# Mix, routing and experts in one block: logits and squares computed tile by tile, the row factor applied later

## The chip, the cores and the metric

One NeuronCore of one Trainium2 chip runs the whole program. The metric is the device time of one execution in microseconds; the kernel before takes 1579.05 us (median of 3 runs, 1575.91 to 1585.28).

## The reference

One inference step of two layers over 264 tokens (256 of a prompt, 8 of decode) of width 1024. Each layer adds four gated branches and then a hierarchical mixture of experts. The change touches the end of the first and the start of the second:

```
proj  = einsum('ntbw,bwd->ntbd', branches, w_branch)      # 4 branches of width 256
gates = sigmoid(gate_raw)                                 # 4 x 1024 a token
x = x + einsum('ntbd,ntbd->ntd', gates, proj) @ w_out

h  = x * rsqrt(mean(x*x) + eps) * norm2_g
pg = softmax(h @ moe_wg + moe_bg)                         # 4 groups, the best one is taken
le = (h @ moe_we + moe_be) of the 8 experts of that group # the best two are taken
e_w = softmax weights of the two, normed to 1, times pg of the group
y = sum over the two of  e_w * (silu(h @ w_gate) * (h @ w_up)) @ w_down   # 1024 -> 256 -> 1024
x = x + y
```

## The kernel before, in words

Activations are kept with features on partitions: `xT`, `hT` are 128 x 8 x 264 (8 tiles of 128 features, 264 tokens). All matrix products are float32 matmuls of TensorE, which the program issues as two instructions each; some operands are split into a high and a low `float32r` part instead, which are multiplied apart.

Each layer is a row of blocks: project, mla, gdn, memory, `mix`, `moe`. A block hands each engine its own list of instructions; engines meet through semaphores, and a barrier of all engines stands between blocks. Loads go out on SyncE's queue (SP) in program order; a wait in that order holds back everything behind it.

`mix` (L1737) loops over the 8 feature tiles `dt`: TensorE multiplies the branches with `w_br` (L1776), VectorE multiplies with the sigmoid of the gates and sums the four branches into `mixT` (L1814 to L1821). Then the output loop (L1784 to L1791) multiplies `mixT` with the 8 tiles of `w_out`, 8 matmuls of 264 columns a tile; VectorE adds each tile to `xT` (L1828). The first four tiles of `w_out` are loaded at the start of the block, tile 4 + i when tile i has been multiplied (L1765).

`moe` (L1847) starts with the loads of the expert weights: pieces of 128 x 1024 floats (512 KB). Tokens are sorted into 48 slots of 32 rows: two of three slots belong to an expert for good (base, 192 pieces of six per slot), the third takes the overflow of whichever expert has more than 32 tokens (96 pieces). Base pieces go round a ring of 21 buffers, overflow pieces round a ring of 3; an overflow piece is loaded only when its slot is used, by a DMA with a condition read from `items` into registers (L1928, L1929, L1931). When a chunk has been multiplied (`chunk_done`), SP issues the base loads that its buffers allow and then the overflow loads.

Ahead of the experts comes a serial chain. VectorE squares `xT` (L2207), TensorE sums over features with a matrix of ones (L1997), ScalarE takes the root, VectorE the reciprocal and `hT = xT * g2 * rstd` (L2213). TensorE computes the 36 logits for three thirds of 88 tokens (L2004), VectorE splits `hT` into high and low (L2217, L2221), TensorE turns the split tiles so that tokens lie on partitions (`split_turn`, L2016, 12 groups of 4 transposes; three groups of four), and ScalarE copies them to `hTM` (L2165). VectorE picks group and experts (`first_max`), TensorE counts tokens per expert and ranks them (L2025, L2029), VectorE finds each token's slot (three `pick`s, L2268, and some small operations) and writes the selection matrix `G` for the first two quads of slots (L2289, L2290). After that come, in TensorE's order, four gathers `hTM` x `G` (L2043), the table of the overflow slots (L2112, computed by VectorE in L2293 to L2299), the transposed slot numbers (L2115), and the first expert chunk. ScalarE copies gathered rows to `HS` (L2174).

The expert stage goes through 12 quads of four slots: four chunks gate/up (L2067), SiLU on ScalarE (L2189), times the up half and the slot's weight `wS` on VectorE (L2339), two transposes (L2076), two chunks down (L2083), `Y` split on ScalarE and VectorE, and 8 matmuls that scatter `Y` back to tokens (L2096), added to `xT` on VectorE (L2332). In between, the gathers for the next two quads run, with `G` from GpSimd (L1967, L1970) and the scatter matrix `Q` from GpSimd (L1978, L1981).

Of the kernel before, what the change touches and what calls it, by code (L numbers as in the profile page):

```python
# [6 lines left out]

# [15 lines left out]
P = 128  # L23
# [43 lines left out]
                  stri=128, sub=1, cols=GCOLS, valid=3, slot=QUADS, quad=QUADS + 1, first=NE, thr=T // W,  # L67
# [25 lines left out]
def constants():  # L93
# [41 lines left out]
    put("first", np.broadcast_to(W * (3 * (e // 2) + e % 2), (P, NE)))  # L135
    put("thr", np.broadcast_to(W * np.arange(1, T // W + 1), (P, T // W)))
# [8 lines left out]
def build(nc, A):  # L145

    with ExitStack() as top:
# [3 lines left out]
        xT = alloc(top, "xT", [P, KT, T])  # L151
        hT = alloc(top, "hT", [P, KT, T])
# [1584 lines left out]
def mix(nc, A, E, l, F):  # L1737

    xT, brT, bank = (E[k] for k in ("xT", "brT", "bank"))
    g0, gT = F["g0"], F["gT"]  # L1740
    with E["Phase"]("mix") as ph:
        S = ph.sem
        w = F["wbr"]
        wo = [ph.sb(f"wo{i}", [P, KT, P]) for i in range(4)]
        mixT = ph.sb("mixT", [P, KT, T])

        def gates(dt, b, n):

            first = 4 * dt + b
            if isinstance(dt, int):  # L1750
                return (g0 if first < MLA_TILES else gT)[:, first % MLA_TILES:first % MLA_TILES + n, :]
            return gT[:, bass.ds(first - MLA_TILES, n), :]

        @ph.b.sync
        def _(sp):
            for i in range(4):
                sp.dma_start(wo[i][:], A["w_out"][l, i]).then_inc(S(f"wo{i}_loaded"), 16)
            with sp.Fori(1, KT // 2) as i:
                for s in range(2):
                    src = A["w_br"][l, 2 * i + s]  # L1760
                    sp.wait_ge(S(f"p{s}_done"), 4 * i)
                    sp.dma_start(w[s][:], src).then_inc(S(f"w{s}_loaded"), 16)
            for i in range(4):
                sp.wait_ge(S("o_done"), i + 1)
                sp.dma_start(wo[i][:], A["w_out"][l, 4 + i]).then_inc(S(f"wo{i}_loaded"), 16)  # L1765

        @ph.b.tensor
        def _(pe):
            def pair(i):
                for s in range(2):  # L1770
                    if not isinstance(i, int):
                        pe.wait_ge(S(f"w{s}_loaded"), 16 * i)
                        pe.wait_ge(S(f"p{s}_read"), 4 * i)
                    for b in range(4):
                        for k in range(2):
                            mm = pe.matmul(bank[4 * s + b][:, 0:T], w[s][:, 2 * b + k, :], brT[:, 2 * b + k, :],  # L1776
                                           start=k == 0, stop=k == 1)
                        mm.then_inc(S(f"p{s}_done"), 1)

            pair(0)  # L1780
            with pe.Fori(1, KT // 2) as i:
                pair(i)
            pe.wait_ge(S("mix_ready"), KT)
            for dt in range(KT):  # L1784
                i = dt % 4
                pe.wait_ge(S(f"wo{i}_loaded"), 16 * (dt // 4) + 16)
                if dt >= 4:
                    pe.wait_ge(S("x_ready"), dt - 3)
                for k in range(KT):
                    mm = pe.matmul(bank[i][:, 0:T], wo[i][:, k, :], mixT[:, k, :], start=k == 0, stop=k == KT - 1)  # L1790
                mm.then_inc(S("o_done"), 1)  # L1791

        @ph.b.scalar
        def _(act):
            def sigmoid(dt):
                nc.scalar.activation(gates(dt, 0, 4), gates(dt, 0, 4), ACT.Sigmoid).then_inc(S("gates_ready"), 1)
# [644 lines left out]
```

## Time and profile before

| | |
|---|---|
| median of 3 runs | 1579.05 us |
| the profiled execution | 1595.82 us, span 1594.0 us |
| busy share of the span | PE 83%, PEld 58%, DVE 45%, ACT 20%, POOL 11% |
| granted TensorE clock | 0.914 of full speed |
| moved by DMA | 307.93 MB, mean 193 GB/s |

PE is TensorE's matmuls, PEld its weight loads, DVE VectorE, ACT ScalarE, POOL GpSimd, SPq the queue of SyncE. The clock is a share of full speed; its two levels are 1.2 and 2.4 GHz. The two layers run the same program, and the span covers both; the first layer's output loop begins at 478.4 us and its experts end at 799.0.

### The profile page before, as it was taken

To read this page: it belongs to the slowest core of one execution; us is meant where nothing else is said; L and a number is where in the kernel's file an instruction comes from. 1 tells how busy PE (TensorE), PEld (TensorE's weight loads), DVE (VectorE), ACT (ScalarE), POOL (GpSimd) and SP (SyncE) were. 2 spreads that over 40 slices of the span, in tenths; PEclk is the share of its full clock that TensorE was granted. 3 is DMA by queue.
4 is the path that set the end of the run, shared out by engine and by line. 5 is a ranking of instruction groups with operands and counts; after the bars stand their busy time and mean duration, and the time that the engine had idled before them with its cause. 6 is when DMAs were issued, how large, how long until landed. Compare 5 with 4: busy or idle time off the path is not lost. (4 is left out here: it accounts for less than half of the span.)

```text
span 1594.0 us, 23230 instructions
## 1 busy us (share of the span) xinstructions
PE 1330.4 (83%) x8322; PEld 928.4 (58%) x8322; DVE 724.4 (45%) x1479; ACT 318.6 (20%) x610; POOL 176.7 (11%) x182
## 2 busy tenths in 40 slices
PE   5968978977889799888879689789788888897886
PEld 2946856966467644343249468579665775443342
DVE  3654766365451612222247547564654534222222
ACT  0212614111120221111111126131111203111110
POOL 0040000000000133330000400000000002333310
PEclk9998989978899699999979989899789997999999
DMA  5462022126133589999734520221261356899995
GB/s 190 150 207 66 1 44 80 53 79 234 58 132 110 229 331 409 408 408 408 288 118 159 198 66 0 55 70 53 79 245 47 132 177 231 343 408 409 408 408 234
DMA packets 89962, 307.93 MB, mean 193 GB/s; under 512 B 16368, under 2 KB 19200, under 8 KB 88192
## 3 DMA queue, kind: packets, MB, share of 16 engines
q1 hardware_dynamic: 86784, 296.08, 49.9%
q0 software_dynamic: 3072, 10.49, 1.9%
q8 instruction: 60, 0.98, 0.3%
q14 instruction: 46, 0.38, 0.1%
HBM read 403.21 MB, written 3.98 MB: 255 GB/s over the span
## 5 line engine op out<-in xcount | busy, mean ns | idle before, releaser
L499 PE MATMUL bank<-hT,wf 128*128 128x264 f32 x1024 | 254.5, 407 | 34.7 <-PEq L202 19.5
L499 PEld LDWEIGHTS bank<-hT,wf 128*128 128x128 f32 x1024 | 203.6, 202 | 78.7 <-issue 26.5
L2067 PE MATMUL bank<-moe_wover,moe_scr 128*32 128x512 f32 x512 | 193.2, 632 | 34.4 <-DMA moe_wover<-in_w_gu 34.1
L2067 PE MATMUL bank<-moe_wbase,moe_scr 128*32 128x512 f32 x1024 | 194.2, 622 | 5.1 <-DMA moe_wover<-in_w_gu 5.1
L2332 DVE TENSOR_TENSOR xT<-xT,bank 128x264 f32<-128x264 f32 x192 | 73.4, 425 | 168.1 <-PE bank L2096 168.1
L2043 PEld LDWEIGHTS bank<-moe_G,moe_hTM 88*128 88x128 f32 x576 | 81.5, 209 | 82.2 <-issue 68.4
L2043 PE MATMUL bank<-moe_G,moe_hTM 88*128 88x256 f32 x576 | 99.2, 316 | 11.7 <-DVE moe_G L2290 9.0
L2083 PE MATMUL bank<-moe_wover,moe_acT 128*32 128x512 f32 x256 | 91.8, 607 | 14.0 <-DMA moe_wover<-in_w_d 10.3
L2083 PE MATMUL bank<-moe_wbase,moe_acT 128*32 128x512 f32 x512 | 91.9, 613 | 9.9 <-ACT moe_acT L2194 6.5
L267 DVE TENSOR_TENSOR moe_Y<-bank,moe_Y 128x512 fp32r<-128x512 f32 x48 | 30.9, 686 | 137.2 <-ACT moe_Y L2197 137.2
L1960 POOL MEMSET moe_wover<- 128x3072 f32 x2 | 5.3, 2658 | 792.4 <-DMA wf<-in_w_gate 792.4
L2174 ACT COPY moe_scr<-bank 128x256 f32<-128x256 f32 x96 | 35.8, 372 | 227.8 <-PE bank L2043 227.8
L2067 PEld LDWEIGHTS bank<-moe_wover,moe_scr 128*32 128x32 f32 x512 | 40.4, 113 | 66.2 <-issue 65.3
L2067 PEld LDWEIGHTS bank<-moe_wbase,moe_scr 128*32 128x32 f32 x1024 | 41.7, 112 | 60.7 <-issue 54.3
L1978 POOL TENSOR_SCALAR moe_Gt<-moe_rows,cst 128x528 f32<-128x528 f32 x24 | 38.5, 1602 | 303.7 <-PE bank L2096 291.4
L1776 PE MATMUL bank<-brT,wbr 128*128 128x264 f32 x256 | 62.6, 405 | 7.1 <-PEq L202 4.4
L2096 PE MATMUL bank<-moe_Q,moe_Y 128*128 128x264 f32 x384 | 64.8, 292 | 2.9 <-DVE moe_Y L267 2.8
L273 PE MATMUL bank<-proj_hsp,proj_wsp 128*128 128x264 f32 x224 | 64.6, 288 | 1.9 <-DVE proj_wsp L267 1.9
L1967 POOL TENSOR_SCALAR moe_Gt<-cst,moe_shifted 88x256 f32<-88x256 f32 x60 | 55.5, 935 | 76.4 <-DVE moe_shifted L2306 73.6
L2096 PEld LDWEIGHTS bank<-moe_Q,moe_Y 128*128 128x128 f32 x384 | 52.8, 189 | 19.1 <-issue 11.7
L274 PE MATMUL bank<-proj_hsp,proj_wsp 128*128 128x264 f32 x224 | 63.5, 283 | 0.0
L275 PE MATMUL bank<-proj_hsp,proj_wsp 128*128 128x264 f32 x224 | 63.5, 283 | 0.0
(509 smaller groups left out, 2150.9 us busy)
## 6 DMA issues: line engine op xcount, KB each, us to landing
moe_wbase<-in_w_gu SPq DMA_DIRECT2D x256, 512.0 KB, 12.3
moe_wbase<-in_w_d SPq DMA_DIRECT2D x128, 512.0 KB, 12.6
moe_wover<-in_w_gu SPq DMA_DIRECT2D x128, 512.0 KB
wf<-in_w_gate SPq DMA_DIRECT2D x64, 512.0 KB, 3.5
moe_wover<-in_w_d SPq DMA_DIRECT2D x64, 512.0 KB
proj_wfm<-in_w_fm SPq DMA_DIRECT2D x28, 512.0 KB, 3.4
wbr<-in_w_br SPq DMA_DIRECT2D x16, 512.0 KB, 3.5
mix_wo<-in_w_out SPq DMA_DIRECT2D x16, 512.0 KB, 5.0
```

The lines of the kernel that those rows point to most:

```text
L273: pe.matmul(out, wh, xh, start=start, stop=False)
L274: pe.matmul(out, wh, xl, start=False, stop=False)
L275: return pe.matmul(out, wl, xh, start=False, stop=stop)
L499: mm = pe.matmul(E["bank"][to][:, 0:T], F["wf"][slot][:, k, :], E["hT"][:, k, :], start=k == 0, stop=k == KT - 1)
L1776: mm = pe.matmul(bank[4 * s + b][:, 0:T], w[s][:, 2 * b + k, :], brT[:, 2 * b + k, :], start=k == 0, stop=k == 1)
L1967: nc.gpsimd.tensor_scalar(Gt[0:n, i, 0:GCOLS], C("cols")[0:n], shifted[0:n, g, i, c:c + 1], None, ALU.is_equal).then_inc(S("gt_ready"), 1)
L1978: nc.gpsimd.tensor_scalar(Gt[:], rows[:], C("slot")[:, q:q + 1], None, ALU.is_equal)\
L2043: mm = pe.matmul(bank[to][:, 0:GCOLS], h[0:n, c, P * k:P * k + P], G[g % 2][0:n, c, :], start=part == 0 and c == 0, stop=part == 1 and c == 2)
L2067: mm = pe.matmul(bank[0][W * p:W * p + W, :], HS[q // GROUP % 2][:, k, at + W * p:at + W * p + W], w[p][:, 512 * (k % 2):512 * (k % 2) + 5 ...
L2083: mm = pe.matmul(bank[2 + half][W * p:W * p + W, :], acT[:, f, W * p:W * p + W], w[p][:, 512 * half:512 * half + 512], start=f == 0, stop= ...
L2096: mm = pe.matmul(bank[4 + n % 3][:, 0:T], Y[part][:, P * d:P * d + P], Q[:, q % 2, :], start=part == 0, stop=part == 1)
L2332: tt(x, x, bank[4 + n % 3][:, 0:T], ALU.add).then_inc(S("x_ready"), 1)
```

## The change

`mix` and `moe` become one block, `tail`, without a barrier between them. The features of the new `x` are scaled by the gain alone (`xg`), not by the row factor 1/rms. Behind the fourth matmul of each output tile, TensorE adds the previous tile's contribution to a 37 x 264 sum: 36 logits of `xg`, and the sum of squares in row 37 (`logits`). `xg` is split and half of the transpose groups run inside the loop. The 37 rows are then turned to tokens on partitions, and the row factor is applied to the logits there; later it enters as a second set of slot weights: SiLU takes it as its scale, and the weight that multiplies the up half contains it as well. The gather goes by thirds as `G` is written. The overflow table is computed on GpSimd right after the offsets, its matmul stands before the gather, and the conditional loads move from SP to ScalarE. The base pieces are loaded in the output loop, into memory that gates and branches held; the memory of `w_out` is later that of the overflow pieces, and `mixT` uses `hT`.

```diff
-def mix(nc, A, E, l, F):
+def tail(nc, A, E, l, F):
...
+            sp.dma_start(wrt[:], A["w_rt"][l]).then_inc(S("wrt_loaded"), 16)
             for i in range(4):
                 sp.dma_start(wo[i][:], A["w_out"][l, i]).then_inc(S(f"wo{i}_loaded"), 16)
...
+            sp.wait_ge(S("mix_ready"), KT)
             for i in range(4):
                 sp.wait_ge(S("o_done"), i + 1)
                 sp.dma_start(wo[i][:], A["w_out"][l, 4 + i]).then_inc(S(f"wo{i}_loaded"), 16)
+                for nb in range(5 * i, 5 * i + 5):
+                    load(nb)
+            for nb in range(20, BASE_RING):
+                load(nb)
...
+        def _(pool):
+            pool.wait_ge(S("o_done"), KT)
+            nc.gpsimd.memset(wover[:], 0.0).then_inc(S("cleared"), 1)
+            pool.wait_ge(S("off_ready"), 2)
+            nc.gpsimd.tensor_tensor(ncnt[:, 2:3], ncnt[:, 3:4], ncnt[:, 1:2], ALU.add).then_inc(S("table_step"), 1)
...
+            nc.gpsimd.tensor_scalar(table[:, 0], table[:, 1], C("eidx")[0:NE], None, ALU.mult)\
+                .then_inc(S("table_ready"), 1)
...
+            def logits(k):
+                pe.wait_ge(S("sq_ready"), k + 1)
+                pe.matmul(bank[4][0:37, 0:T], last[:], sq[:, k % 2, :], start=k == 0, stop=False).then_inc(S("ss_done"), 1)
+                pe.wait_ge(S("xg_ready"), k + 1)
+                pe.matmul(bank[4][0:37, 0:T], wrt[:, k, :], xg[:, k % 3, :], start=False, stop=k == KT - 1).then_inc(S("lg_done"), 1)
...
             pe.wait_ge(S("mix_ready"), KT)
+            pe.wait_ge(S("wrt_loaded"), 16)
+            pe.wait_ge(S("zeroed"), 1)
             for dt in range(KT):
...
                 for k in range(KT):
                     mm = pe.matmul(bank[i][:, 0:T], wo[i][:, k, :], mixT[:, k, :], start=k == 0, stop=k == KT - 1)
+                    if k == 3 and dt:
+                        logits(dt - 1)
                 mm.then_inc(S("o_done"), 1)
+                if 4 <= dt < 7:
+                    split_turn(2 * dt - 8)
+                    split_turn(2 * dt - 7)
+            logits(KT - 1)
+            split_turn(6)
+            pe.wait_ge(S("lgT_ready"), 1)
             for c, (t0, n) in enumerate(THIRDS):
+                mm = pe.transpose(bank[4][0:n, 37 * c:37 * c + 37], lgT[:, t0:t0 + n], ident[0:37, 0:37])
+            mm.then_inc(S("lgT_done"), 1)
+            for b in range(7, 12):
+                split_turn(b)
...
-            split_turn(2)
+            pe.wait_ge(S("table_ready"), 1)
+            pe.matmul(bank[1][:, 0:2 * OVER], ones[0:NE, :], table[:].rearrange("p a b -> p (a b)"), start=True,
+                      stop=True).then_inc(S("items_done"), 1)
...
-            pe.wait_ge(S("G_ready"), 3)
             pe.wait_ge(S("hTM_ready"), 12)
-            for k in range(4):
-                gather(0, k, 4 + k)
-            pe.wait_ge(S("table_ready"), 1)
...
+            for c, (t0, n) in enumerate(THIRDS):
+                pe.wait_ge(S("G_ready"), c + 1)
+                for k in range(4):
+                    for part, h in enumerate(hTM):
+                        mm = pe.matmul(bank[4 + k][:, 0:GCOLS], h[0:n, c, P * k:P * k + P], G[0][0:n, c, :],
+                                       start=part + c == 0, stop=part + c == 3)
...
+            nc.scalar.activation(rs[:, 3:4], E["epsc"][:], ACT.Sqrt)
+            for dt in range(KT):
+                act.wait_ge(S("res_ready"), dt + 1)
...
+                nc.scalar.activation(sq[:, dt % 2, :], xT[:, dt, :], ACT.Square).then_inc(S("sq_ready"), 1)
+                if 4 <= dt < 7:
+                    turned(2 * dt - 8)
+                    turned(2 * dt - 7)
...
+            def refill(n):
+                act.wait_ge(S("chunk_done"), n + 1)
+                for i in range(OVER_RING, len(over_pieces)):
+                    if last_user(over_pieces[i - OVER_RING]) == n:
+                        load(i)
+            act.wait_ge(S("items_ready"), 1)
+            act.wait_ge(S("cleared"), 1)
+            for i in range(OVER_RING):
+                load(i)
             for k in range(KT):
                 gathered(0, k, 4 + k % 4)
+                if k == 5:
+                    refill(0)
+            refill(1)
...
+                for c in range(3 if q else 0):
+                    if more:
                         gathered(g + 1, 4 * (q % GROUP) + c, 7)
+                    refill(STEPS * q + c)
+                if q == 0:
+                    refill(2)
+                    act.wait_ge(S("wS_ready"), 1)
                 act.wait_ge(S("chunk_done"), STEPS * q + 4)
-                nc.scalar.activation(sg[:], bank[0][:, 0:256], ACT.Silu).then_inc(S("silu_done"), 1)
+                nc.scalar.activation(sg[:], bank[0][:, 0:256], ACT.Silu, scale=wS[:, 1, q:q + 1])\
+                    .then_inc(S("silu_done"), 1)
...
+            for dt in range(KT):
+                dve.wait_ge(S("o_done"), dt + 1)
+                x = xT[:, dt, :]
+                tt(x, x, bank[dt % 4][:, 0:T], ALU.add).then_inc(S("res_ready"), 1)
...
+                ts(xg[:, dt % 3, :], x, V("g2", dt), None, ALU.mult).then_inc(S("xg_ready"), 1)
...
+                high_part(nc, hsp[0][:, dt, :], xg[:, dt % 3, :]).then_inc(S("h_high"), 1)
...
+                low_part(v, hsp[1][:, dt, :], xg[:, dt % 3, :], hsp[0][:, dt, :]).then_inc(S("h_split"), 1)
+            step(v.tensor_copy(lgT[:], bank[4][0:37, 0:T]), "lgT_ready", wait=False)
+            dve.wait_ge(S("root_ready"), 1)
+            step(v.reciprocal(rs[some, 0:3], rs[some, 0:3]))
...
-            step(tt(ohg[:], ohg[:], C("valid").unsqueeze(2).to_broadcast([P, 3, 4]), ALU.mult))
             for i in range(2):
-                for c in range(3):
-                    step(tt(OH[:, i, c].rearrange("p (g e) -> p g e", g=4),
-                            ohg[:, c].unsqueeze(2).to_broadcast([P, 4, 8]),
-                            oh[i][:, c].unsqueeze(1).to_broadcast([P, 4, 8]), ALU.mult), wait=i + c == 3)
+                step(tt(OH[:, i].rearrange("p c (g e) -> p c g e", g=4),
+                        ohg[:].unsqueeze(3).to_broadcast([P, 3, 4, 8]),
+                        oh[i][:].unsqueeze(2).to_broadcast([P, 3, 4, 8]), ALU.mult), wait=i == 1)
...
-PHASES = [branches, moe]
+PHASES = [branches]
```

## Rows read from the trace of the kernel before

**Rows 1.** Windows, layer 0: us, busy time (instructions) by engine, PEclk, DMA share, GB/s.
```profile
478.40:508.90 30.50, 30.44 (x128) 25.35 (x128) 3.02 (x8) 0.00 (x0) 0.00 (x0) 0.94 0.24 70
...
542.90:552.00 9.10, 6.54 (x31) 5.89 (x32) 3.44 (x18) 1.49 (x4) 1.54 (x2) 0.50 0.00 0
...
566.20:579.60 13.40, 11.51 (x74) 6.91 (x74) 0.65 (x2) 2.46 (x7) 11.41 (x13) 0.75 0.67 247
579.60:785.20 205.60, 177.66 (x1416) 80.19 (x1408) 51.15 (x116) 32.77 (x78) 46.36 (x47) 0.97 1.02 405
785.20:799.00 13.80, 10.57 (x78) 4.89 (x74) 6.11 (x15) 1.83 (x4) 0.00 (x0) 1.00 0.04 17
```

**Rows 2.** Timeline, output loop to turning, layer 1: start, length, operation, [idle before, releaser].
```profile
1278.45 0.43 DVE L1828 TENSOR_TENSOR xT<-xT,bank 128x264 f32<-128x264 f32 x1 [3.13 <-PE bank L1790]
...
1299.81 0.43 DVE L1828 TENSOR_TENSOR xT<-xT,bank 128x264 f32<-128x264 f32 x1 [3.13 <-PE bank L1790]
...
1317.34 0.19 DVE L2224 TENSOR_TENSOR moe_lg<-bank,row 88x36 f32<-88x36 f32 x1 [1.34 <-PE bank L2004]
...
1325.23 1.95 PE L2016 MATMUL bank<-cst,moe_scr 128*88 128x128 f32 x16
```

**Rows 3.** Groups by line and form, VectorE: busy us, mean ns of one.
```profile
L1555 DVE TENSOR_SCALAR gdn_y<-zT,vec 128x264 f32<-128x264 f32 x12 | 3.4, 351 | 5.6 <-PEq L202 5.6
...
L2269 DVE TENSOR_REDUCE moe_tq<-moe_Aq 128x6 f32<-128x192 f32 x6 | 2.1, 353 | 0.2
```

**Rows 4.** Timeline, logits to the first expert chunk, layer 0.
```profile
528.09 0.19 DVE L2224 TENSOR_TENSOR moe_lg<-bank,row 88x36 f32<-88x36 f32 x1 [1.33 <-PE bank L2004]
...
532.70 0.70 DVE L2250 TENSOR_TENSOR moe_OH<-moe_ohg,moe_oh 128x32 f32<-128x32 f32 x6
...
540.51 0.48 DVE L2290 SCALAR_TENSOR_TENSOR moe_G<-cst,moe_tq,moe_Gt 88x256 fp32r<-88x256 f32 x1
...
542.32 0.48 DVE L2290 SCALAR_TENSOR_TENSOR moe_G<-cst,moe_tq,moe_Gt 88x256 fp32r<-88x256 f32 x1
...
542.85 5.49 PE L2043 MATMUL bank<-moe_G,moe_hTM 88*128 88x256 f32 x24 [4.02 <-DVE moe_G L2290]
...
548.83 0.60 PE L2115 MATMUL bank<-cst,moe_tq 88*2 88x88 f32 x3
549.47 0.42 DVE L2301 COPY moe_tokT<-bank 2x264 f32<-2x264 f32 x1 [5.34 <-PE bank L2115]
...
551.67 0.81 SPq L1931 DMA_DIRECT2D moe_wover<-in_w_gu  x3
...
551.99 1.07 PE L2067 MATMUL bank<-moe_wbase,moe_scr 128*32 128x512 f32 x2 [2.56 <-DMA moe_wover<-in_w_gu]
```

**Rows 5.** Timeline, layer 0: the table on VectorE, GpSimd's first and third pair.
```profile
543.19 0.22 DVE L2296 TENSOR_SCALAR moe_table<-cst,moe_ncnt 32x16 f32<-32x16 f32 x1
...
550.46 2.28 POOL L1967 TENSOR_SCALAR moe_Gt<-cst,moe_shifted 88x256 f32<-88x256 f32 x2 [37.65 <-DVE moe_shifted L2306]
...
556.45 1.82 POOL L1967 TENSOR_SCALAR moe_Gt<-cst,moe_shifted 88x256 f32<-88x256 f32 x2
```

**Rows 6.** Chain of work that ended last, layer 1, first and second expert chunk.
```profile
1341.26 3.64 PE bank L2067 x16
...
1346.92 1.85 PE bank L2067 x16
```

**Rows 7.** Timeline, end of the experts, layer 0.
```profile
775.01 0.08 SPq L1931 DMA_DIRECT2D moe_wover<-in_w_d  x1
775.17 0.59 PE L2083 MATMUL bank<-moe_wbase,moe_acT 128*32 128x512 f32 x1 [1.80 <-DMA moe_wover<-in_w_d]
...
796.08 2.89 DVE L2332 TENSOR_TENSOR xT<-xT,bank 128x264 f32<-128x264 f32 x8
```

**Rows 8.** Timeline, first SiLU, layer 0: the table load, the slot weights.
```profile
565.13 1.28 ACT L2189 ACT_TABLE_LOAD   x1
...
567.75 0.17 DVE L2327 COPY moe_wS<-bank 128x12 f32<-128x12 f32 x1 [13.88 <-PE bank L2133]
```

More of the change, by code:

```diff
@@ L8 @@
+import math
 from contextlib import ExitStack
@@ L1863, in moe, with at @@
     over_at = {x: i for i, x in enumerate(over_pieces)}
[L1864 removed]
+    with E["Phase"]("tail") as ph:
         S = ph.sem
[L1866 to L1868 removed]
+        where = [-(-F["at"] // 32) * 32]
+        def at(name, shape, dt=F32):
+            t = nc.alloc_sbuf_tensor_at(f"tail_{name}", shape, dt, offset=where[0])
+            where[0] += -(-4 * math.prod(shape[1:]) // 32) * 32
+            return t
+        wbase = at("wbase", [P, BASE_RING, D_MODEL])
+        where[0] = -(-max(where[0], F["end"]) // 32) * 32
+        again = where[0]
+        wo = [at(f"wo{i}", [P, KT, P]) for i in range(4)]
+        above = where[0]
+        mixT = hT
+        where[0] = again
+        wover = at("wover", [P, OVER_RING, D_MODEL])
+        sg = at("sg", [P, 256])
+        ac = at("ac", [P, 256])
+        acT = at("acT", [P, 2, P])
+        assert where[0] <= above
+        where[0] = above
+        Y = [nc.alloc_sbuf_tensor_at(f"tail_Y{i}", [P, D_MODEL], F32R, offset=E["hT_at"] + 4 * D_MODEL * i)
+             for i in range(2)]
+        scr = at("scr", [P, 2 * KT * T])
@@ new lines, in tail @@
+        Q = at("Q", [P, 2, T], F32R)
+        rows = at("rows", [P, 2, T])
+        wS = at("wS", [P, 2, QUADS])
+        rs = at("rs", [P, 4])
+        last = at("last", [P, 37])
+        lgT = at("lgT", [37, T])
+        wrt = at("wrt", [P, KT, 37])
+        lg = at("lg", [P, 3, 36])
+        m = at("m", [P, 8, 3])
+        eg = at("eg", [P, 3, 4])
+        ohg = at("ohg", [P, 3, 4])
+        sel = at("sel", [P, 3, 4, 8])
+        le = at("le", [P, 3, 8])
+        oh = [at(f"oh{i}", [P, 3, 8]) for i in range(2)]
@@ L2020, in _, with pair @@
-            pe.wait_ge(S("h_split"), 4)
-            split_turn(0)
-            split_turn(1)
+            def pair(i):
+                for s in range(2):
+                    if not isinstance(i, int):
+                        pe.wait_ge(S(f"w{s}_loaded"), 16 * i)
+                        pe.wait_ge(S(f"p{s}_read"), 4 * i)
+                    for b in range(4):
+                        for k in range(2):
+                            mm = pe.matmul(bank[4 * s + b][:, 0:T], w[s][:, 2 * b + k, :], brT[:, 2 * b + k, :],
+                                           start=k == 0, stop=k == 1)
+                        mm.then_inc(S(f"p{s}_done"), 1)
@@ L2348, in _, with branches @@
                 add(KT * (QUADS - 1) + d)
-PHASES = [branches, moe]
+def branches(nc, A, E, l):
+    with ExitStack() as shared:
+        sb = lambda name, shape: E["alloc"](shared, name, shape, F32)
+        base = nc.sbuf_base
+        g0 = sb("g0", [P, MLA_TILES, T])
+        E = dict(E, zT=sb("zT", [P, FM_N, T]), tm=sb("tm", [P, 3, TM_W]), brT=sb("brT", [P, 8, T]))
+        F = dict(g0=g0, wf=[sb(f"wf{i}", [P, KT, P]) for i in range(2)])
+        project(nc, A, E, l, F)
+        mla(nc, A, E, l, dict(F, gT=g0, at=0))
+        F.update(gT=sb("gT", [P, GATE_TILES - MLA_TILES, T]), memT=sb("memT", [P, KT, MEM]))
+        gdn(nc, A, E, l, dict(F, at=0))
+        F.update(wbr=[sb(f"wbr{i}", [P, 8, P]) for i in range(2)])
+        F.update(end=nc.sbuf_base)
+        memory(nc, A, E, l, dict(F, at=GDN_TILES))
+        tail(nc, A, E, l, dict(F, at=base))
+PHASES = [branches]
 OUTS = dict(
```

434 lines of the change are left out of this document (181 added, 253 removed).

## The prediction

> **What bounds the kernel now.** I read the windows over the stages of the first layer first, then the timelines around the hand-over from the output loop to the experts, then the chain of waits for the second layer. From the first refill to the last landing, 205.6 us of the expert stage run with the 16 DMA engines fully busy at 405 GB/s, while TensorE is busy 177.66 us of it [rows 1]: the stream of expert weights sets this stage. Ahead of it the stream stands still: between 542.9 and 552.0 nothing moves [rows 1], because the ring of 21 base pieces is full and no expert chunk has been computed. So the end of a layer follows the moment at which the first expert chunk frees a buffer; everything that brings this chunk forward by 1 us brings the end forward by 1 us, as long as the stream behind it is the same. That chunk stands at the end of one serial chain: output loop, barrier, square sums, logits, routing on VectorE, gather, overflow table, loads. After the last landing 13.8 us of computing are left [rows 1].
>
> **Output loop to logits.** The loop goes at 3.56 us a tile (0.43 of the residual add and 3.13 idle before it) [rows 2], so 16 instructions at 0.2225. In layer 0 loop start to biased logits is 478.4 to 528.28, 49.9 us [rows 1, 4]; in layer 1 the loop ends at 1299.81, started 28.5 earlier, and the logits end at 1317.53: 46.2 us [rows 2]. All square sums, the normalisation, its split and the old logits lie in that.
> The change puts two more matmuls of 264 columns behind each tile but the last: 4 instructions, 0.89 us, seven times, 6.2 us on TensorE's own path. Six of the twelve transpose groups move into the loop as well, 24 transposes at 1.95/16 = 0.12 [rows 2], 3.0 us. VectorE does four operations of 264 columns per tile (0.43, 0.35 [rows 3], two more of that kind) and ScalarE one square and at times two copies, under 2 us of each 4.45 us tile: hidden behind TensorE. After the last tile stand the add 0.43, the gain 0.35, two matmuls 0.89, the copy out of PSUM 0.42 [rows 4], three small transposes, one copy and the root on ScalarE, reciprocal, scale and bias, with some eight hand-overs of 0.1: 4.6 us, between 4 and 6.5 (the upper end if ScalarE has to load its table once more, 1.28 [rows 8]). New length: layer 0 30.4 + 6.2 + 3.0 + 4.6 = 44.2, a gain of 5.7; layer 1 28.5 + 6.2 + 3.0 + 4.6 = 42.3, a gain of 3.9. Together 9.6.
> Against it: TensorE now waits for two memsets on VectorE before the loop, 0.35, and the routing weights stand first on SP's queue and push the w_br loads back by 0.35: 1.4 for both layers.
> SP's queue in the loop: the second half of w_out goes out one tile at a time with five base pieces of 512 KB behind each, 1.3 us a piece at the 405 GB/s of the full stream [rows 1]. The last w_out piece lies behind 18 others and lands some 30 us into the loop; its tile starts at 33. This hides it by 3 us. The window of the loop shows 70 GB/s now [rows 1], so there is room. That the base pieces come 30 us earlier is worth nothing by itself: the ring is full before routing ends in both kernels.
>
> **Routing to the first expert chunk.** The mask and six one-hot writes (0.70 [rows 4]) become two wider writes: 0.4 gained, bounds 0 to 0.9. Six slot operations shrink to four, one copy is added: 0.35 gained, bounds 0 to 0.6. The gather now starts on the first third of G instead of the third: 540.51 + 0.48 = 540.99 instead of 542.80 [rows 4]. From 540.99 - 0.75 = 540.24 its 24 matmuls take 5.49, to 545.7; the three transposes 0.60, to 546.4. Before, the table matmul stood behind the gather, then the copies to integers, SP's register loads and its issue at 551.67, and the first expert matmul ran at 551.99 [rows 4]. Now the table is done while VectorE builds G, and ScalarE, idle there, issues the loads. Gain 5.6 a layer, 11.2 together.
> What this hangs on is GpSimd. Five operations of 16 columns on it, each waiting for the one before, precede the table matmul (0.56), and TensorE stands in order behind that matmul, with the whole gather. VectorE meanwhile has two picks (0.35 for each half [rows 3]), six small operations and the first pair of G, some 3.4 us. No row has such an operation on GpSimd: VectorE's for the same table is 0.22, GpSimd's for 256 columns is 1.14 or 0.91 [rows 5]. That gives 1.6 to 6.2 us with hand-overs, so a loss of 0 to 3.4 a layer. 16 columns are nearer to the small one: I take 2.5 us and no loss.
> The pair of GpSimd at 550.46, beside a busy VectorE, took 2.28; the pair at 556.45, beside an idle one, 1.82 [rows 5]. The Trainium skill, page "SBUF — State Buffer", section "SBUF: two separate sides", says that VectorE in some kinds of operation and GpSimd lock one shared port pair for a whole instruction; by the rule each of the five could wait for one VectorE operation, about 1.7 us in all, and the table would still come about with G; by the row the price is 0.23 an operation. The trace agrees in sign; neither changes the sum.
> Clock: the first chunk runs at half clock in both layers, 3.64 us for 16 matmuls against 1.85 soon after [rows 6], after 2.5 us without work for TensorE. That pause goes. Gain 0 to 2.6 a layer with the gathers beside it; I take 1.3, together 2.6.
> First SiLU: ScalarE now waits for the slot weights (567.92) before it; the table load that stood at 565.13 [rows 8] may come behind this wait, and the gathers' copies behind that: 0 to 1.3 lost a layer, 0.6 taken, together 1.2.
>
> **Expert stage.** The same pieces at the same rate: no change over 205.6 us. ScalarE gets 96 conditional loads a layer, and 16 times two register loads. Behind each stand its own copies of gathered rows, SiLU, Y. In a quad with two overflow slots the load for the next chunk is issued behind a gather's copy, so TensorE may wait some 0.5 us, 12 times, 6 us a layer, beside 27.9 us of slack: hidden by the stream.
> The tail is different. SP issues the overflow loads in order behind base loads that it can't place: one came out at 775.01 and TensorE, idle for 1.80 us, started at 775.17 [rows 7]. So TensorE is several chunks behind the stream when it ends at 785.2. On ScalarE's queue a skipped load is done at once, and TensorE can follow the landings: the last down chunk and part of the one before, 3 us, and 5.4 of Y, its low part and the combine (the last eight adds alone 2.89 [rows 7]) give 8.4 after the last landing, instead of 13.8: up to 5.4, or nothing if TensorE is late for other reasons. I take 3 a layer, together 6.
>
> **Sum.** 9.6 - 1.4 + 11.2 (which holds the 0.75 a layer of the routing) + 2.6 - 1.2 + 6 = 26.8, say 27 us of the profiled execution's 1595.82 (span 1594.0). That execution is 1% above the median of the runs, 1579.05; I take the difference off the median: 1552. With every term at its low end 5 us are left, with every one at its high end 38.
>
> **Rivals.**
> *Given back before the experts* (about 1573): GpSimd at its upper price (6.8 for both layers), ScalarE's table load behind the root (2.6) and behind the slot weights (1.4 more), nothing from the tail (6), the clock (2.6) or the shorter routing (1.5): 20.9 of the 27 are gone. For it: TensorE is in order behind the table; against it: 256 columns are no measure for 16. Chance 0.13.
> *The clock falls in the expert stage* (slower, 1605). Now that TensorE isn't held in lumps, it would follow the stream in small gaps. Place: the 205.6 us of each layer. Price: a chunk at half clock takes 3.64 for 1.85 [rows 6], so each us at half clock costs 0.5. It decides from 56 us a layer on, where the slack of 27.9 is used up; at half the stage, 103 us, it costs 23.5 a layer: 47 less the 21 that are left of the gain. For it: from 566.2 to 579.6 TensorE was busy 11.51 of 13.4 us and the granted clock was 0.75, between its levels of 1.2 and 2.4 GHz. Against it: over the long stage it was busy the same share and had 0.97 [rows 1]. The Trainium skill, page "TensorE: Matmul & The Clock Gate", section "HAM oscillation — how this bites in real kernels", has this mechanism: a kernel that waits for DMA between bursts of matmuls loses its clock again and again. The trace has it in the one stretch and not in the other. Chance 0.07.
> *ScalarE becomes the bound* (about 1590): if a conditional load cost it over 0.7 us in the chain of each chunk, 27.9 us of slack over 40 chunks would be gone. SP's three loads took 0.81 [rows 4], so 0.27 each. Chance 0.08.
>
> **How the numbers follow.** Forecast 0.72, its own range 1544 to 1571. The range of 1541 to 1577 takes in most of the first rival and holds some 8 in 10. Within 0.5% of 1579 (1571 to 1587) is what a measurement of this kernel can't tell from no change: faster 0.77, the same 0.12, slower 0.11.
>
> **What will show it.** The output loop with 4.45 us between its adds; first add after the loop to biased logits under 6 us; the first expert matmul some 10 us sooner after the loop's start; DMA idle only in routing; 205 us of full DMA as before; 8 to 9 us after the last landing. Wrong if the table matmul starts after the first third of G, if TensorE's waits for base pieces come with a clock under 0.9 in the long stage, or if that stage is longer than 208 us.

## The result, and the profile after

The changed kernel takes 1573.22 us (median of 20 runs, 1560.37 to 1583.53), the kernel before, run beside it, 1582.56 us (20 runs): ratio 0.9942, interval 0.9919 to 0.9964. It is faster by 9 us (0.6%), not by the 27 of the forecast. The profiled execution took 1580.17 us (span 1578.4) against 1595.82: 15.6 us between the spans. The stretches that the change touches hold 9.2 of these. Another 7.5 lie in the blocks ahead of them, whose code is the same: the first branch matmul comes 3.1 us earlier in layer 0, and in layer 1 4.4 us more than the end of layer 0 did. Behind the experts of layer 1, 1.1 us are lost again.

Windows of layer 0 after, columns as in [rows 1] (busy time of PE, PEld, DVE, ACT, POOL, then PEclk, DMA share, GB/s):

```profile
440.70:478.50 37.80, 32.89 (x128) 26.13 (x129) 22.31 (x53) 10.62 (x11) 0.00 (x0) 0.91 0.44 143
478.50:520.00 41.50, 41.48 (x180) 29.84 (x180) 10.74 (x29) 5.83 (x13) 0.00 (x0) 0.96 0.80 316
520.00:526.40 6.40, 3.95 (x18) 2.40 (x18) 4.57 (x8) 1.32 (x4) 2.66 (x1) 0.78 0.00 0
526.40:538.40 12.00, 6.49 (x40) 5.86 (x38) 8.49 (x43) 4.17 (x8) 1.51 (x5) 0.64 0.01 1
538.40:545.30 6.90, 5.95 (x30) 5.49 (x30) 2.59 (x8) 1.46 (x4) 0.00 (x0) 0.50 0.00 0
545.30:565.00 19.70, 18.32 (x124) 10.21 (x124) 5.18 (x21) 5.05 (x12) 15.47 (x17) 0.85 0.78 292
565.00:573.00 8.00, 7.49 (x44) 3.10 (x48) 0.00 (x0) 0.74 (x2) 5.00 (x6) 0.60 0.29 94
573.00:777.50 204.50, 177.38 (x1432) 81.16 (x1424) 51.94 (x118) 33.73 (x78) 46.46 (x47) 1.00 1.02 407
777.50:789.04 11.54, 8.24 (x58) 3.96 (x54) 5.34 (x13) 1.92 (x4) 0.00 (x0) 1.00 0.05 20
```

One line for each stretch of the serial path: branch tiles, output loop, end of the logits, routing, gather, first quad (two lines), stream, tail. The loop has TensorE busy for all of its 41.5 us; the stream runs as before, at 407 GB/s with the full clock.

The same stretches, cut at the starts of instructions in the timelines (the biased logits and the experts at their ends), in us for layer 0 / layer 1; forecast and measured are gains over both layers:

| stretch | before | after | forecast | measured |
|---|---|---|---|---|
| first branch matmul to first output matmul | 34.6 / 34.5 | 37.8 / 37.8 | -1.4 | -6.5 |
| to the last residual add | 30.5 / 28.8 | 41.5 / 41.5 | -18.4 | -23.8 |
| to the biased logits | 19.4 / 17.7 | 6.4 / 6.4 | +27.9 | +24.4 |
| to VectorE's first operation for G | 11.8 / 11.9 | 12.0 / 12.0 | +1.5 | -0.3 |
| to the first expert matmul | 11.9 / 11.9 | 6.8 / 6.8 | +9.7 | +10.0 |
| to the end of the experts | 247.0 / 245.7 | 243.8 / 243.4 | +7.4 | +5.5 |
| sum | 355.2 / 350.5 | 348.3 / 348.0 | +26.7 | +9.2 |

Timeline after, end of the output loop in layer 0:

```profile
520.06 0.43 DVE L2251 TENSOR_TENSOR xT<-xT,bank 128x264 f32<-128x264 f32 x1 [4.02 <-PE bank L1970]
520.09 2.66 POOL L1881 MEMSET tail_wover<- 128x3072 f32 x1 [401.81 <-PE bank L1970]
520.53 2.37 DVE L2255 TENSOR_SCALAR tail_xg<-xT,vec 128x264 f32<-128x264 f32 x1
522.95 0.64 PE L1944 MATMUL bank<-tail_xg,tail_wrt 128*37 128x264 f32 x2 [1.31 <-DVE tail_xg L2255]
523.75 1.08 PE L1954 MATMUL bank<-cst,tail_scr 128*88 128x128 f32 x4 [0.16 <-DVE tail_scr L270]
526.15 0.27 DVE L2267 TENSOR_TENSOR tail_lg<-tail_lg,row 88x108 f32<-88x108 f32 x1
```

The last gain operation takes 2.37 us, where the same operation takes 0.36 in the loop. GpSimd's memset of the overflow buffers began beside it, also released by the last output tile.

### The profile page after: what moved, and what is told of

Same layout as the page of the kernel before. It is cut to its first block and busy times, and to the rows that moved or that the text cites. A ratio compares the mean times of both kernels' runs of the same rounds, so it can differ in the third digit from the quotient of the medians.

```text
span 1578.4 us, 23156 instructions
## 1 busy us (share of the span) xinstructions
PE 1331.3 (84%) x8264; PEld 921.3 (58%) x8264; DVE 722.7 (46%) x1485; ACT 327.1 (21%) x628; POOL 183.0 (12%) x192
## 3 DMA queue, kind: packets, MB, share of 16 engines
q0 software_dynamic: 3072, 10.49, 1.9%
## 5 line engine op out<-in xcount | busy, mean ns | idle before, releaser
L2032 PE MATMUL bank<-tail_wbase,tail_scr 128*32 128x512 f32 x1024 | 186.4, 604 | 21.2 <-DMA tail_wbase<-in_w_gu 21.2
L2032 PE MATMUL bank<-tail_wover,tail_scr 128*32 128x512 f32 x512 | 185.4, 601 | 4.5 <-DMA tail_wbase<-in_w_gu 4.5
L2048 PE MATMUL bank<-tail_wbase,tail_acT 128*32 128x512 f32 x512 | 94.9, 622 | 22.2 <-DMA tail_wbase<-in_w_d 14.7
L2008 PEld LDWEIGHTS bank<-tail_G,tail_hTM 88*128 88x128 f32 x528 | 70.3, 196 | 68.5 <-issue 64.1
L2048 PE MATMUL bank<-tail_wover,tail_acT 128*32 128x512 f32 x256 | 94.6, 613 | 7.6 <-ACT tail_acT L2210 3.8
L2008 PE MATMUL bank<-tail_G,tail_hTM 88*128 88x256 f32 x528 | 87.8, 305 | 2.8 <-ACT tail_scr L2160 2.8
L1970 PE MATMUL bank<-hT,tail_wo 128*128 128x264 f32 x256 | 65.6, 408 | 4.7 <-DVE tail_last L2244 4.7
L2061 PE MATMUL bank<-tail_Q,tail_Y 128*128 128x264 f32 x384 | 65.5, 295 | 2.9 <-DVE tail_Y L270 2.8
L1935 PEld LDWEIGHTS bank<-brT,wbr 128*128 128x128 f32 x256 | 52.5, 208 | 22.3 <-issue 12.2
L2061 PEld LDWEIGHTS bank<-tail_Q,tail_Y 128*128 128x128 f32 x384 | 53.8, 191 | 18.9 <-issue 11.7
```

The costliest lines, as they stand in the source:

```text
L2008: mm = pe.matmul(bank[to][:, 0:GCOLS], h[0:n, c, P * k:P * k + P], G[g % 2][0:n, c, :], start=part == 0 and c == 0, stop=part == 1 and c == 2)
L2032: mm = pe.matmul(bank[0][W * p:W * p + W, :], HS[q // GROUP % 2][:, k, at + W * p:at + W * p + W], w[p][:, 512 * (k % 2):512 * (k % 2) + 5 ...
L2048: mm = pe.matmul(bank[2 + half][W * p:W * p + W, :], acT[:, f, W * p:W * p + W], w[p][:, 512 * half:512 * half + 512], start=f == 0, stop= ...
L2061: mm = pe.matmul(bank[4 + n % 3][:, 0:T], Y[part][:, P * d:P * d + P], Q[:, q % 2, :], start=part == 0, stop=part == 1)
```

## The experiments

All change the changed kernel unless said; ratios are against the kernel before, run on the same chip. Where a whole time can't separate two kernels, the stretches of the table do; each is read from one execution with two layers.

**The changed kernel again.**

> The changed kernel itself once more, beside the others on the same chip, for the size of what the parts gave: 0.994 of the time before, first branch matmul to the end of the experts 348 us in each layer. If its routing counts at full clock in this execution (1.9 instead of 3.3 us), 1.4 less.

1575.22 us, 0.9952 (0.9923 to 0.9981). From the first branch matmul to the end of the experts (branch to end, below) 346.9 / 346.8. Counting, from the one-hot rows to the ranks, took 3.27 us in layer 0 and 1.90 in layer 1; the branch stretch 36.5 and 38.2: these two move with the granted clock from one execution to the next.

**Routing weights last.**

```diff
-            sp.dma_start(wrt[:], A["w_rt"][l]).then_inc(S("wrt_loaded"), 16)
             for i in range(4):
                 sp.dma_start(wo[i][:], A["w_out"][l, i]).then_inc(S(f"wo{i}_loaded"), 16)
             with sp.Fori(1, KT // 2) as i:
...
+            sp.dma_start(wrt[:], A["w_rt"][l]).then_inc(S("wrt_loaded"), 16)
             sp.wait_ge(S("mix_ready"), KT)
```

> The changed kernel with one load moved: the routing weights (148 KB in 148-byte rows) go out behind the branch-weight refills instead of ahead of w_out. Theory (the load holds back the refills): the second pair of branch tiles waits 2.24 us in the changed kernel and runs at half clock (9.07 us instead of 7.38); without the load ahead the wait falls to the 0.9 to 1.1 us of the kernel before and the second pair to 7.4, so first branch matmul to first output matmul is 35.0 us instead of 37.8 in both layers, some 5.5 us in all: 1567 to 1568. Rival (the refills are held by the four w_out tiles alone, the changed kernel's longer wait has another cause): the wait stays over 2 us, the time at 1573.

1566.38 us, 0.9928 (0.9900 to 0.9957). Timeline of the branch tiles in layer 0, first the changed kernel, then this one:

```profile
440.79 0.33 SPq L1850 DMA_DIRECT2D tail_wrt<-in_w_rt  x1
...
451.99 9.03 PE L1935 MATMUL bank<-brT,wbr 128*128 128x264 f32 x32 [2.24 <-DMA wbr<-in_w_br]
```

```profile
444.82 14.97 PE L1935 MATMUL bank<-brT,wbr 128*128 128x264 f32 x64 [0.96 <-DMA wbr<-in_w_br]
```

In layer 0 the wait falls to 0.96, and two pairs of tiles take 14.97, where one took 9.03 in the changed kernel. In layer 1 the wait is long, 2.76, but only because the first pair ran at full clock there (7.36 us instead of 9.04):

```profile
1212.46 7.36 PE L1935 MATMUL bank<-brT,wbr 128*128 128x264 f32 x32 [2.09 <-PEq L205]
1222.58 22.68 PE L1935 MATMUL bank<-brT,wbr 128*128 128x264 f32 x96 [2.76 <-DMA wbr<-in_w_br]
```

In both layers the second pair begins 10.0 to 10.1 us after the first, as in the kernel before (9.9 to 10.2); in the eight runs that have the load ahead it is 10.5 to 12.6, in the changed kernel 11.3. The stretch is 34.9 / 35.1, as in the kernel before. So the load costs what its landing delays, and what TensorE's clock loses in the wait, not its 0.33 us of issue. The share of the clock differs between executions: in the changed kernel run again, layer 0, the second pair waited 2.71 us and still ran at full clock (7.38). Counting, too, ran at full clock in both layers (1.90). The rows of this load are not of 148 bytes: the array holds the 8 x 37 floats of a partition in one piece, 1184 bytes.

**Clearing in the loop.**

```diff
-            pool.wait_ge(S("o_done"), KT)
-            nc.gpsimd.memset(wover[:], 0.0).then_inc(S("cleared"), 1)
+            for i in range(OVER_RING):
+                pool.wait_ge(S("o_done"), 5 + i)
+                nc.gpsimd.memset(wover[:, i], 0.0).then_inc(S("cleared"), 1)
```

> The changed kernel, with GpSimd's clearing of the three overflow buffers cut into three pieces of 1024 columns, each behind the output tile that used this memory last (the fifth, sixth and seventh), instead of one piece of 3072 behind the eighth. Theory (GpSimd's memset holds VectorE's gain operation that starts beside it): the last xg takes 0.36 us instead of 2.37, last add to biased logits 4.4 us instead of 6.36, 2 us a layer, 4 in all: 1569; single operations inside the loop get longer by up to 0.9 and stay hidden. Rival (the last xg is long because it waits for something else): 2.37 stays, 1573.

1568.43 us, 0.9940 (0.9910 to 0.9969): as a whole not to be told from the changed kernel. In the profiled execution the branch stretch of layer 1, which this edit doesn't touch, took 40.3. The edited stretch is clear: last add to biased logits 4.18 in both layers, 2.2 less. Timeline of layer 0, a tile with a memset and the last:

```profile
501.95 0.95 POOL L1882 MEMSET tail_wover<- 128x1024 f32 x1 [387.74 <-PE bank L1971]
...
502.39 0.66 DVE L2256 TENSOR_SCALAR tail_xg<-xT,vec 128x264 f32<-128x264 f32 x1
...
519.33 0.36 DVE L2256 TENSOR_SCALAR tail_xg<-xT,vec 128x264 f32<-128x264 f32 x1
```

Each piece beside a gain operation lengthens it, to 0.66; alone it takes 0.36. In both kernels it ends 0.15 us after the memset does (522.90 after 522.75; 503.05 after 502.90). The Trainium skill, page "SBUF — State Buffer", section "SBUF: two separate sides", says that the port pair shared by GpSimd and VectorE (in some of VectorE's kinds of operation) is locked for a whole instruction by whichever of the two engines starts first; by that rule VectorE waits out the memset, and these rows agree, but for the end: 0.15 us behind the memset is less than the 0.36 that the operation takes alone.

**All turns behind the logits.**

```diff
-                if 4 <= dt < 7:
-                    split_turn(2 * dt - 8)
-                    split_turn(2 * dt - 7)
             logits(KT - 1)
-            split_turn(6)
...
-            for b in range(7, 12):
+            for b in range(12):
                 split_turn(b)
```

> The changed kernel with all twelve transpose groups behind the three small transposes of the logits, none in the output loop and none ahead of the logits. Theory (they cost TensorE's path there, and behind the logits TensorE has nothing else to do): output loop 41.5 to 38.9 us, the group ahead of the small transposes gives 0.7, and counts and ranks run at full clock (1.83 us instead of 3.2) because TensorE works right up to them: 4.7 us a layer, 9 in all, 1564. Rival (TensorE, at half clock, gets through twelve groups only after VectorE has its one-hot rows, and counting starts late): first half gained, 1 to 2 us a layer given back, 1568 to 1570. Rival 2 (the loop was bound by the loads of w_out and pieces): loop stays at 41.5, 1573.

1565.54 us, 0.9908 (0.9876 to 0.9941). Loop 37.2 / 39.4 (full clock / first tiles at half clock), last add to logits 5.5 instead of 6.4, counting 1.90 / 1.89. Timeline of layer 0:

```profile
522.38 5.90 PE L1954 MATMUL bank<-cst,tail_scr 128*88 128x128 f32 x48
...
528.54 0.35 PE L1984 MATMUL bank<-ones,tail_both 88*32 88x1 f32 x6 [0.27 <-DVE tail_both L2286]
```

The twelve groups fit between the logits and the one-hot rows; TensorE then stands idle for 0.27 us instead of 2.98, and counts at full clock. With the turns in the loop, in seven runs, counting ran at full clock throughout in 4 of 14 layers, at half in 5; with all turns behind the logits, in five runs, at full in all ten.

**Overflow loads back on SP.**

```diff
-                act.dma_start(wover[:, i % OVER_RING], source(e, c), cond=used)
+                sp.dma_start(wover[:, i % OVER_RING], source(e, c), cond=used)
```

(with the order of SP of the kernel before)

> The changed kernel with the conditional overflow loads back on SP, in the order of the kernel before; all else as changed. Theory (ScalarE's queue lets TensorE follow the landings): the tail after the last landing goes back from 11.5 to 13.8 us in the first layer, TensorE's waits for base pieces turn into waits for overflow loads again: 2 to 3 us a layer slower, 1577 to 1579. Rival (the loads on ScalarE cost as much as they give, they stand ahead of its copies in the first quads): the same within 2 us, 1572 to 1575. Rival 2 (they hold up ScalarE more than they give): faster, 1568.

1578.07 us, 0.9987 (0.9960 to 1.0015). First expert matmul to the end 246.9 / 245.5, as before the change (247.0 / 245.7). TensorE's waits by releaser (us, times, longest), changed kernel, then this one:

```profile
PE bank L2032 <- DMA tail_wbase<-in_w_gu: 25.7, 28, 1.9
PE bank L2048 <- DMA tail_wbase<-in_w_d: 14.7, 10, 1.8
```

```profile
PE bank L2051 <- DMA tail_wover<-in_w_gu: 31.1, 21, 6.1
PE bank L2067 <- DMA tail_wover<-in_w_d: 12.6, 9, 1.7
```

So without the move to ScalarE the expert stage keeps only 0.3 of the 5.5 us that it gained.

**Wide weights.**

```diff
-        last = at("last", [P, 37])
+        last = at("last", [P, P])
-        wrt = at("wrt", [P, KT, 37])
+        wrt = at("wrt", [P, KT, P])
```

(columns 37 to 127 cleared at the start of the block)

> The changed kernel with the weights of the logits and of the square sums padded with zeros to 128 columns (two buffers of xg instead of three to make room). In the changed kernel a tile with logits takes 4.77 us: 16 w_out instructions 3.76 and four for the logits 1.01, against 3.56 and 0.89 at the pace of the loop before. Theory (weights of 37 columns break the row of weight loads that TensorE does beside its matmuls): padded, a tile takes 4.45, the loop 39.3 instead of 41.5, 2.2 us a layer. Rival (the break comes from the change of the sum's bank, whatever the width): 4.77 stays.

1563.20 us, 0.9887 (0.9852 to 0.9922). Timeline of TensorE over one tile of the loop, changed kernel, then this one:

```profile
490.49 0.64 PE L1942 MATMUL bank<-tail_sq,tail_last 128*37 128x264 f32 x2
490.96 0.61 PE L1944 MATMUL bank<-tail_xg,tail_wrt 128*37 128x264 f32 x2
491.50 3.83 PE L1970 MATMUL bank<-hT,tail_wo 128*128 128x264 f32 x16
495.26 0.64 PE L1942 MATMUL bank<-tail_sq,tail_last 128*37 128x264 f32 x2
```

```profile
489.49 0.61 PE L1943 MATMUL bank<-tail_sq,tail_last 128*128 128x264 f32 x2
489.94 0.61 PE L1945 MATMUL bank<-tail_xg,tail_wrt 128*128 128x264 f32 x2
490.38 3.72 PE L1972 MATMUL bank<-hT,tail_wo 128*128 128x264 f32 x16
493.94 0.61 PE L1943 MATMUL bank<-tail_sq,tail_last 128*128 128x264 f32 x2
```

Start to start 4.77 and 4.45 us. Wider weights are faster: the four instructions take 0.89 instead of 1.01, and the w_out matmuls around them 3.56 instead of 3.76. Loop 39.3 / 37.6 (layer 1 at full clock from its start). The starts of single matmuls in the trace put the loss at the changes of width: they follow each other by 0.22 us in both kernels, but in the changed one by 0.32 into the narrow weights, 0.25 behind the first narrow one, 0.32 out of them and 0.33 behind the first wide one; with wide weights it is 0.22 throughout. Why a change of width costs this is not settled. The Trainium skill, page "TensorE: Matmul & The Clock Gate", section "Weight-path perf modes — Fast Weight Load (FWL) and DoubleRow", gives the fast load to 128 weights that are not float32; by that rule float32 weights get no fast load at either width, and here the width made 0.32 us a tile.

**Squares summed on VectorE.**

```diff
+                if 0 < dt < KT - 1:
+                    tt(acc[:], acc[:], sq[:, dt % 2, :], ALU.add).then_inc(S("acc_done"), 1)
...
+                if k >= KT - 2:
                     pe.matmul(bank[4][0:37, 0:T], last[:], acc[:] if k < KT - 1 else sq[:, k % 2, :], start=False,
                               stop=False)
```

> The changed kernel, in which VectorE adds the squares of the first seven tiles up (one more operation of 264 columns, 0.43 us, in each tile from the second) and TensorE sums two squared tiles over features instead of eight. Theory (each logits pair stands on TensorE's own path, VectorE has room): six square matmuls of 0.47 us leave the loop, a tile takes 4.3 us instead of 4.77, the loop 38.7 instead of 41.5, 2.8 us a layer, 5.6 in all. Rival (the price is that of breaking the row of w_out matmuls, not of what stands in the break): a tile loses under 0.3. Rival 2 (VectorE, with some 2.4 us of work and its waits in each tile, becomes late): the last add to biased logits gets longer than 6.4.

1563.87 us, 0.9902 (0.9866 to 0.9938). TensorE in the loop of layer 0:

```profile
491.12 0.64 PE L1947 MATMUL bank<-tail_xg,tail_wrt 128*37 128x264 f32 x2
491.69 3.83 PE L1973 MATMUL bank<-hT,tail_wo 128*128 128x264 f32 x16
495.44 0.64 PE L1947 MATMUL bank<-tail_xg,tail_wrt 128*37 128x264 f32 x2
```

A tile takes 4.32 us, the loop 37.6 / 39.6; last add to logits 5.9 / 6.6. VectorE had the room: its operations behind the last add take as long as in the changed kernel, and the 6.6 of layer 1 come from TensorE at half clock. The tile also shows what the narrow weights cost: 18 instructions at 0.2225 are 4.00, so half as many narrow instructions, with as many changes of width, cost the same 0.32.

**Filling TensorE's pauses** (on top of all turns behind the logits).

```diff
+            for _ in range(22):
+                pe.transpose(bank[4][:, 0:P], ident, ident)
             pe.wait_ge(S("table_ready"), 1)
...
+            for _ in range(8):
+                pe.transpose(bank[4][:, 0:P], ident, ident)
             pe.wait_ge(S("hTM_ready"), 12)
```

> The kernel with all turns behind the logits, in addition TensorE turns the unit matrix 22 times while it waits for the overflow table and 8 times between the table and the gather; the results are used by nothing. Theory (the gather runs at half clock because TensorE has nothing to do ahead of it): the gather's 24 matmuls take 3.6 us (bound by the thirds of G) instead of 5.46 and the first chunk 1.9 instead of 2.9 to 3.6, first G to first chunk 4.3 to 5 us instead of 6.84; 3 us a layer, 6 in all against that kernel. Rival (the clock stays low, the 22 take 5 us and push the table and the gather back): first G to first chunk 8 to 9 us, 4 us in all slower than that kernel.

1552.94 us, 0.9841 (0.9798 to 0.9885), against 0.9908 without the filling. The window over the gather of layer 0 (PEclk is the third number from the end):

```profile
530.00:533.10 3.10, 3.03 (x26) 3.04 (x27) 1.71 (x5) 0.00 (x0) 0.00 (x0) 1.00 0.00 0
```

The gather takes 3.06 us at full clock instead of 5.46 at half; first G to first expert matmul 5.2 instead of 6.8, of which 0.9 is now a wait for ScalarE's copies.

**All of it.** Diffs as above (without wide weights and filling), the first refills ahead of w_out, the small memsets ahead of the branch tiles.

> All of what paid put together: the changed kernel with the first branch refills ahead of w_out and the routing weights last, the clearing in the loop in three pieces, all turns behind the logits, squares summed on VectorE, and the small memsets ahead of the branch loop. Theory (the parts lie on one serial path and add up): first branch matmul to first output matmul 34 us, loop 36.4 (34.7 at full clock throughout), last add to biased logits 3.5, counting at full clock; pair to end of experts 334 us a layer instead of 348, so 28 us in all less than the changed kernel, 1545. Rival (what the one part gives the clock takes back, pauses now fall together): 338 to 342 a layer, 1555 to 1560.

1558.62 us, 0.9864 (0.9827 to 0.9902); branch to end 341.1 / 342.1, as the rival had it. Timeline of layer 0:

```profile
457.46 7.38 PE L1941 MATMUL bank<-brT,wbr 128*128 128x264 f32 x32 [3.05 <-DMA wbr<-in_w_br]
...
506.23 3.15 PE L1978 MATMUL bank<-hT,tail_wo 128*128 128x264 f32 x8 [2.10 <-DMA tail_wo<-in_w_out]
```

The four w_out tiles now delay the second refill, and in the shorter loop a w_out piece behind the base pieces comes late: the cover of 3 us that the prediction counted is gone. After that wait 8 instructions took 3.15 us instead of 2.05.

**All of it, loads spread.**

```diff
+            for i in range(1, KT // 2):
...
+                for x in ((0, 1), (2, 3), ())[i - 1]:
+                    sp.dma_start(wo[x][:], A["w_out"][l, x]).then_inc(S(f"wo{x}_loaded"), 16)
...
-                for nb in range(5 * i, 5 * i + 5):
+                for nb in range(2 * i, 2 * i + 2):
```

> All parts together once more, with what the last runs showed: routing weights and square-sum weights padded to 128 columns, squares summed on VectorE, all turns behind the logits, the clearing in the loop, small memsets early, routing weights last, w_out two tiles behind each of the first two pairs of branch refills, and two base pieces instead of five behind each w_out tile of the loop (the rest behind the loop). Theory (the terms of the path add up once no load is late in them): first branch to first output matmul 33 to 34 us, loop 32 to 34, last add to biased logits 3.5, counting 1.9, first G to first chunk 6.84, experts 243.5: 330 a layer against 348 for the changed kernel, so 36 us less in all, 1537. Rival (shorter stages make their loads late and TensorE's clock falls in the gaps, as in the run before): 338 a layer, 1553.

1546.04 us, 0.9776 (0.9750 to 0.9802). Branch stretch 34.9 / 35.0, loop 33.2 / 34.9, logits 4.0 in both layers, but from the one-hot rows to the ranks 3.0 / 3.1 again; branch to end 332.7 / 335.7, between theory and rival. Timeline of layer 0:

```profile
512.66 7.37 PE L1959 MATMUL bank<-cst,tail_scr 128*88 128x128 f32 x48
...
519.96 0.35 PE L1990 MATMUL bank<-ones,tail_both 88*32 88x1 f32 x6
```

Counting itself ran at full clock (1.8 us from 519.96 on), but it began 1.2 us late in both layers: the twelve groups ran at a clock of 0.77 and took 7.37 and 7.42 us instead of 5.90. That is the rival named for the run with all turns behind the logits.

**And filled.**

> The same, with TensorE turning the unit matrix into a bank that nothing reads: 22 times ahead of the overflow table, 8 ahead of the gather, and 5 behind each of the four gathers of the first quad and behind its turn. Theory (the clock falls in the short pauses and costs more than the filling): first G to first chunk 5.2 us instead of 6.84, first quad's second half at full clock, first chunk to the end 240 instead of 243.5: 5 us a layer less than the kernel without filling, 1527. Rival (the first quad's gathers wait for ScalarE's copies, and the filling only stands in line): first chunk to the end stays at 243, only 1.6 a layer gained, 1534.

**1536.01 us, 0.9719 (0.9696 to 0.9743)**: the fastest kernel here, 45 us under the kernel before. The filling gave the 10 us that the theory named, from 1546 and not from 1537. First expert matmul to the end 240.2 / 240.0, against 241.9 / 243.1 without the filling; branch to end 330.8 / 327.9. Windows of layer 0, gather, first quad's two halves, stream:

```profile
526.40:531.40 5.00, 5.00 (x39) 4.40 (x37) 2.37 (x7) 0.69 (x3) 0.00 (x0) 0.92 0.00 0
531.40:545.00 13.60, 13.59 (x109) 7.17 (x110) 4.69 (x20) 4.09 (x10) 10.78 (x12) 1.00 0.78 283
545.00:556.00 11.00, 11.00 (x97) 7.04 (x95) 1.22 (x3) 3.26 (x8) 9.70 (x11) 1.00 0.73 276
556.00:760.00 204.00, 175.85 (x1420) 80.66 (x1416) 51.22 (x117) 32.66 (x76) 46.49 (x47) 1.00 1.02 406
```

## Why the prediction was wrong

The structure was right: the first expert chunk came earlier, the stream ran as before, each layer's end followed. Its terms were mis-sized, by 17.5 us in all, and nearly always to the same side. The largest misses are the price of the logits in the loop and that of the load ahead of the branch refills.

- **Output loop: 18.4 forecast, 23.8 measured.** The step that failed priced the four added instructions at the loop's own pace, 0.2225 us [rows 2]. With 37 columns of weights between 128 the two changes of width cost 0.32 more a tile; at 128 columns the tile takes the forecast 4.45 to the hundredth. That is 7 x 0.32 = 2.2 a layer. Another 1.7 is in layer 1: before, its loop began at full clock, after at 0.62 (1260.05 to 1264.50 us). The turns were priced right (2.6 against 3.0).
- **Branch tiles: 1.4 forecast, 6.5 measured.** The load ahead of the refills was priced by its issue on SP. It delays their landing; TensorE waits 2.24 instead of 1.13 us in layer 0 and starts the second pair at half clock (0.81 over the pair), 1.65 more. The wait for the memsets was right (2.34 against 1.97).
- **Last add to logits: 4.6 a layer forecast, 6.4 measured.** The eight hand-overs were counted, not the GpSimd instruction that the last output tile releases together with them. The prediction had the port rule in hand and tried it on the table alone. Without the memset it takes 4.18. Inside that, the one turn ahead of the small transposes is another 0.9, as the run with all turns behind shows.
- **Routing: 1.5 gained forecast, 0.3 lost.** VectorE's savings came (12.0 us with counting at half clock, 10.6 at full). TensorE lost turns that had kept it busy up to the counting: 3.27 us instead of 1.90 in both layers of this execution, though not in every one. The step moved work into the loop as a cost alone and did not ask what the clock would do where it had been.
- **Gather, table, loads: 9.7 forecast, 10.0 measured.** GpSimd's five operations took 1.8 us (2.5 taken), and the table's matmul began 1.4 us ahead of the first third of G. The gather stayed at half clock.
- **Expert stage: 7.4 forecast, 5.5 measured.** With the loads back on SP all but 0.3 of it is gone. The forecast read its tail of 13.8 us from 785.2 on as "after the last landing", but data still moved until 788.0. Windows around the end of the loads of layer 0, before, then after:

```profile
787.50:788.00 0.50, 0.50 (x5) 0.21 (x2) 0.00 (x0) 0.07 (x1) 0.00 (x0) 1.00 0.06 25
788.00:789.00 1.00, 0.67 (x5) 0.46 (x5) 0.66 (x2) 0.31 (x1) 0.00 (x0) 1.00 0.00 0
```

```profile
779.50:780.00 0.50, 0.16 (x4) 0.17 (x8) 0.05 (x1) 0.28 (x1) 0.00 (x0) 1.00 0.06 25
780.00:781.00 1.00, 1.00 (x12) 0.29 (x8) 0.00 (x0) 0.00 (x0) 0.00 (x0) 1.00 0.00 0
```

From the last data to the end of the experts it was 11.0 / 10.0 us and is 9.0 / 9.3: 2.7 gained of the 6. The other 2.8 lie ahead of the last data. There the first chunk went from 3.64 to 2.99, half of the 1.3 taken, and the stall behind the first quad stayed: from 565 to 573 us hardly anything was loaded, 94 GB/s at a clock of 0.60, because the buffers of the gate/up chunks were loaded again and no down chunk had freed one yet [rows 1 has the later part of the same pause before]. "DMA idle only in routing" was wrong.

The rivals: the clock did not fall in the stream (1.00, TensorE busy 177.4 of 204.5 us), and ScalarE was no bound. The time of "given back before the experts" came true, its mechanism did not: neither the table nor the root's table load cost anything. The clock took its share ahead of the experts, where the prediction had looked for gains only. So the 1573 lies in the stated range by luck: the range reached that far to take in this rival. Of the signs named, the stream came as forecast; 4.77 us between the adds, 6.4 to the logits, and a first expert matmul only 6.8 / 3.5 us sooner after the loop's start did not.

## What to carry to other kernels

Price a load that is put ahead in a queue by the landing it delays and by the clock that TensorE can lose in the wait, and a wait on an event by everything else that the same event starts. Work that is moved out of a pause leaves the pause: where the granted clock is at its lower level, ask what will keep TensorE busy, or fill the pause with work that nobody reads. Pad narrow weights that stand between wide ones and measure it: here the price lay at each change of width. When stages get shorter, look again at which load, and which work of TensorE, had been hidden behind them.

## What was not expected of the hardware

A memset of 128 x 3072 on GpSimd (2.66 us) held a VectorE operation of 0.36 us for 2.37. Weights of 128 columns instead of 37 for 4 of 20 matmuls made the row of them faster, 4.45 against 4.77 us, all of it at the two changes of width. With thirty transposes a layer that nothing reads the kernel went from 0.9908 to 0.9841 of the time before. Of that 3.3 us stand in the stretch that they fill (6.84 to 5.20 and 5.14) and 2.4 between the first expert matmul and the end (244.1 / 243.2 to 243.0 / 241.8); the rest lies in stretches whose clock moves between executions.
